# A hybrid attention and pooling step: h by column chunks, four resident weight blocks, w_out split by chunks

## The reference

```python
mod = silu(c) @ w_ada + b_ada                 # shift, scale, gate: 3 x 1024 for each sequence
h = layer_norm(x) * (1 + scale) + shift
q, k, v, g_attn, u, g_pool = split(h @ w_in)  # w_in: 1024 x 2304
q, k = rope(q), rope(k)
o_attn = windowed attention with sinks        # 8 q heads, 2 kv heads, own chunk of 64 and 2 before it
o_pool = (trailing means of u over 2/4/8/16 rows - u) @ w_pool * pool_scale
mixed = concat([o_attn * silu(g_attn), o_pool * silu(g_pool)])
y = mixed @ w_out                             # w_out: 1024 x 1024
out = layer_norm(alpha * x + gate * y) * ln_g + ln_b
```

## Time and profile before

| | |
|---|---|
| Median of 3 runs | 482.06 us (481.42 to 482.42) |
| Span of the profiled execution | 479.1 us (its own time is given by this span alone) |
| PE | busy 447.9 us (93%), 2598 matmuls |
| PE weight loads | 376.8 us (79%) |
| VectorE | 279.3 us (58%) |
| ScalarE | 129.8 us (27%) |
| GpSimd | 118.4 us (25%) |
| Chain that ended last | PE 83%, DVE 9%, ACT 2%, issue 2%, DMA 2% |
| DMA | 46.30 MB, 97 GB/s over the span, 418 GB/s at most |

### The profile page before, as it was taken

One profiled execution on the slowest core, in us unless ns is written; L12 is line 12 of the kernel. 1 busy time (PEld: TensorE's weight loads), 2 busy tenths in 40 slices (PEclk: granted clock), 3 DMA queues, 4 the chain that ended last, 5 costly groups with the idle time before them and its releaser, 6 DMA issues.

```text
span 479.1 us, 6605 instructions
## 1 busy us (share of the span) xinstructions
PE 447.9 (93%) x2598; PEld 376.8 (79%) x2598; DVE 279.3 (58%) x524; ACT 129.8 (27%) x307; POOL 118.4 (25%) x83
## 2 busy tenths in 40 slices
...
GB/s 308 415 418 274 219 0 1 219 2 275 44 46 131 45 44 7 49 46 1 50 8 46 5 45 10 41 51 0 183 16 73 88 89 88 89 88 90 88 98 79
DMA packets 22545, 46.30 MB, mean 97 GB/s; under 512 B 11089, under 2 KB 13649, under 8 KB 21202
## 3 DMA queue, kind: packets, MB, share of 16 engines
...
...
## 4 chain that ended last, share of the span: by engine, by line
PE 83%; DVE 9%; ACT 2%; issue 2%; DMA 2%; POOL 0%; SPq 0%; DVEq 0%; POOLq 0%
PE proj_ps L579 15%; PE proj_ps L581 14%; PE proj_ps L580 14%; PE proj_ps L706 6%; PE proj_ps L707 6%; PE proj_ps L708 6%; PE s_ps L612 3%; PE t_ps L640 2%; PE o_ps L662 2%; PE o_ps L663 2%; PE s_ps L515 2%; DMA xs<-x_all 2%; DVE wo_lo L1126 2%; PE t_ps L535 2%; DVE xnT L989 2%
## 5 line engine op out<-in xcount | busy, mean ns | idle before, releaser
L579 PE MATMUL proj_ps<-h_hi,w_hi 128*128 128x384 f32 x400 | 139.2, 348 | 0.3 <-DVE rt L1024 0.3
L581 PE MATMUL proj_ps<-h_hi,w_lo 128*128 128x384 f32 x400 | 135.0, 338 | 0.0
L580 PE MATMUL proj_ps<-h_lo,w_hi 128*128 128x384 f32 x400 | 135.0, 338 | 0.0
L1250 POOL TENSOR_TENSOR w_lo<-w_raw,w_hi 128x1024 fp32r<-128x1024 f32 x16 | 41.3, 2584 | 160.2 <-ACT w_hi L802 160.2
L579 PEld LDWEIGHTS proj_ps<-h_hi,w_hi 128*128 128x128 f32 x400 | 75.7, 189 | 4.9 <-issue 2.2
L580 PEld LDWEIGHTS proj_ps<-h_lo,w_hi 128*128 128x128 f32 x400 | 75.8, 189 | 0.9
L581 PEld LDWEIGHTS proj_ps<-h_hi,w_lo 128*128 128x128 f32 x400 | 75.6, 189 | 0.0
L706 PE MATMUL proj_ps<-wo_hi,m_hi 128*128 128x512 f32 (+1 forms) x152 | 58.9, 388 | 3.0 <-DVE wo_lo L1126 3.0
L708 PE MATMUL proj_ps<-wo_hi,m_lo 128*128 128x512 f32 (+1 forms) x152 | 58.4, 384 | 0.0
L707 PE MATMUL proj_ps<-wo_lo,m_hi 128*128 128x512 f32 (+1 forms) x152 | 58.4, 384 | 0.0
L1046 DVE SCALAR_TENSOR_TENSOR mixed<-th,proj_ps 128x384 f32<-128x384 f32 x24 | 13.3, 554 | 57.0 <-ACT th L816 57.0
...
## 6 DMA issues: line engine op xcount, KB each, us to landing
w_raw<-w_in SPq DMA_DIRECT2D x18, 512.0 KB, 4.8
...
xs<-x_all SPq DMA_DIRECT2D x9, 512.0 KB, 9.1
xf<-x_all SPq DMA_DIRECT2D x9, 512.0 KB, 4.1
...
y_out<-yr SPq DMA_DIRECT2D x8, 512.0 KB, 2.9
wo_raw<-w_out SPq DMA_DIRECT2D x4, 512.0 KB, 3.3
wo_rest<-w_out SPq DMA_DIRECT2D x4, 512.0 KB, 8.9
```

Of the source, the lines that this page charges most:

```text
L579: pe.matmul(bank[:, 0:CW], w_hi[:, w, k, :], hi, start=(k == 0), stop=False)
L580: pe.matmul(bank[:, 0:CW], w_hi[:, w, k, :], lo, start=False, stop=False)
L581: mm = pe.matmul(bank[:, 0:CW], w_lo[:, w, k, :], hi, start=False, stop=(k == KT - 1))
L1250: pool.tensor_tensor(w_lo[:, b % 2], w_raw[:, b % RAW], w_hi[:, b % 2].bitcast(F32), ALU.subtract).then_inc(wlo_done, 1)
```

## The change

Five things:

1. The two parts of h lie in one tensor `hl`, chunk after chunk (in a chunk: half, part, slice), where they lay in two tensors over all columns. The early modulation slabs are placed to fit.
2. w_in blocks: four high parts are resident, and the low part is written over the raw block. A buffer is refilled when the last unit of block b-4 is done; `W_SPLIT` says after which unit ScalarE splits a block.
3. Loads: slabs 2 and 3 and blocks 2 and 3 come ahead of x tiles 6 to 8.
4. The order: units 4 to 7 are gates of chunks 0 and 1, and chunk 2 of k and v comes as units 8 and 9. Tiles 6 to 8 are transposed after units 4 and 5. The lists of the engines are written to suit; GpSimd makes 2 low parts of h where it made 5.
5. w_out is loaded into the memory of h, slices 0 to 2 when chunk 0 of h has had its last use, 3 to 5 with chunk 1, 6 and 7 with chunk 2; the low part is written over the raw one. Slices 0 to 4 are split before and between the last units. The first two tiles for the residual (`xf`) are loaded before.

The diff, cut to its core:

```diff
-    for c in range(NCH):
+    for c in range(2):
         units += [("k", 0, c), ("v", 0, c)]
-    units += [("ga", j, c) for j in range(4) for c in range(NCH)]
+    units += [("ga", j, c) for j in range(2) for c in range(2)]
+    units += [("k", 0, 2), ("v", 0, 2), ("ga", 0, 2), ("ga", 1, 2)]
+    units += [("ga", j, c) for j in range(2, 4) for c in range(NCH)]
...
+W_SPLIT = {LAST_UNIT[b - RAW] + 1: b for b in range(RAW, NBLK)}
...
-POOL_LOW = [(0, 0), (0, 2), (1, 2), (2, 0), (2, 2)]
+POOL_LOW = [(2, 1), (2, 3)]
...
-POOL_WO = (3, 4)
+POOL_WO = (2, 5)
+WO_CHUNK = [0, 0, 0, 1, 1, 1, 2, 2]
...
-    h_hi = place("h_hi", [P, KT, TOK], F32R, at=r_h)
-    h_lo = place("h_lo", [P, KT, TOK], F32R, at=r_h + KT * TOK * 4)
-    wo_hi = place("wo_hi", [P, KT, D], F32R, at=r_h)
-    wo_lo = place("wo_lo", [P, KT, D], F32R, at=r_h + KT * TOK * 4)
+    hl = place("hl", [P, NCH, 2, 2, KT // 2, CW], F32R, at=r_h)
+    wo = place("wo", [P, KT, 2, D], F32R, at=r_h)
+    wo_raw = place("wo_raw", [P, KT, 2, D], at=r_h)
...
+    wada = [place(f"wada{i}", [P, KT, 512], at=r_h + o * CW * 4) for i, o in enumerate((0, 11, 24, 35))]
...
+    w_lo = place("w_lo", [P, RAW, KT, P], F32R, at=r_raw)
...
+    w_hi = place("w_hi", [P, RAW, KT, P], F32R, at=r_hl)
...
-                    sp.wait_ge(whi_done, b - RAW + 1)
-                    sp.wait_ge(wlo_done, b - RAW + 1)
+                    sp.wait_ge(unit_done, LAST_UNIT[b - RAW] + 1)
                 sp.dma_start(w_raw[:, b % RAW], w_in[b]).then_inc(ld_w[b % RAW], 16)
             def load_w_out(k):
-                if k < RAW:
-                    sp.wait_ge(whi_done, NBLK + k - RAW + 1)
-                    sp.wait_ge(wlo_done, NBLK + k - RAW + 1)
-                elif k == RAW:
-                    sp.wait_ge(s_done, NQ)
-                sp.dma_start(w_out_raw(k), w_out[k]).then_inc(ld_wo[k], 16)
+                sp.wait_ge(unit_done, LAST_USE[WO_CHUNK[k]] + 1)
+                sp.dma_start(wo_raw[:, k, 1, :], w_out[k]).then_inc(ld_wo[k], 16)
+            def load_xf(t):
+                if t >= 2:
+                    sp.wait_ge(r_done, 2 * (t - 1))
+                sp.dma_start(xf[:, t % 2, :], x_all[t]).then_inc(ld_xf[t % 2], 16)
...
+            load_x(3)
             load_w(0)
+            load_x(4)
             load_w(1)
-            load_x(3)
-            load_x(4)
             load_x(5)
+            load_ada(2)
+            load_ada(3)
+            load_w(2)
+            load_w(3)
+            sp.dma_start(cosT[:], cos_d).then_inc(ld_cs, 16)
+            sp.dma_start(sinT[:], sin_d).then_inc(ld_cs, 16)
             load_x(6)
             load_x(7)
             load_x(8)
...
-            for k in range(RAW, KT):
+            for k in range(KT):
                 load_w_out(k)
-            sp.wait_ge(unit_done, LAST_PROJ + 1)
...
-            ada(1, low)
             x_transpose(2)
-            ada(1, high)
             select(0)
+            ada(1)
             select(1)
             unit(0, low)
+            unit(1, low)
             x_transpose(3)
-            unit(1, low)
             x_transpose(4)
             x_transpose(5)
             ada(2)
-            x_transpose(6)
             select(2)
-            ada(3, low)
             unit(2, low)
-            ada(3, high)
-            x_transpose(7)
+            ada(3)
+            unit(3, range(0, 2))
             select(3)
-            x_transpose(8)
-            unit(3, low)
+            unit(3, range(2, 4))
             for n in range(4):
                 unit(n, high)
-            after = {6: [(v_transposes, 0), (v_transposes, 1)], 7: [(ada, 4), (v_transposes, 2), (v_transposes, 3)],
-                     8: [(v_transposes, 4), (v_transposes, 5)], 11: [(ada, 5)]}
+            after = {4: [(x_transpose, 6)], 5: [(x_transpose, 7), (x_transpose, 8)],
+                     10: [(v_transposes, 0), (v_transposes, 1)], 11: [(ada, 4), (v_transposes, 2), (v_transposes, 3)],
+                     12: [(v_transposes, 4), (v_transposes, 5)], 15: [(ada, 5)]}
...
-                if b >= 2:
-                    act.wait_ge(unit_done, LAST_UNIT[b - 2] + 1)
-                act.activation(w_hi[:, b % 2], w_raw[:, b % RAW], ACT.Copy).then_inc(whi_done, 1)
+                if b >= RAW:
+                    act.wait_ge(unit_done, LAST_UNIT[b - RAW] + 1)
+                act.activation(w_hi[:, b % RAW], w_raw[:, b % RAW], ACT.Copy).then_inc(whi_done, 1)
...
             evac_ada(2)
+            h_high(1, (0, 1))
+            evac_ada(3)
+            h_high(0, (2, 3))
+            h_high(1, (2, 3))
+            w_high(2)
+            evac_unit(1)
+            w_high(3)
+            evac_unit(3)
+            normalise(6)
             normalise(7)
-            h_high(1, (0, 1))
+            evac_unit(4)
+            normalise(8)
             evac_xt(6)
-            normalise(8)
-            evac_ada(3)
+            evac_unit(5)
             evac_xt(7)
             evac_xt(8)
-            h_high(0, (2, 3))
-            h_high(1, (2, 3))
-            evac_unit(1)
-            h_high(2)
-            evac_unit(3)
-            w_high(2)
-            evac_unit(5)
-            w_high(3)
-            after = {7: 4, 11: 5}
-            for n in range(6, NU):
+            h_high(2, (0, 1))
+            evac_unit(6)
+            h_high(2, (2, 3))
+            evac_unit(7)
+            after = {11: 4, 15: 5}
+            for n in range(8, NU):
                 b = block_of(n)
                 evac_unit(n)
                 if n in after:
                     evac_ada(after[n])
                 if n == NU - 1:
-                    for k in range(1, 6):
+                    wo_high(5)
+                if UNITS[n] == ("z", GROUPS[3], 0):
+                    mixed_high(0)
+                    for k in range(3):
                         wo_high(k)
+                if n == LAST_PROJ:
+                    wo_high(3)
+                    wo_high(4)
                 for i in SLOTS.get(n, []):
                     slot(i)
-                if b is not None and LAST_UNIT[b] == n and b + 2 < NBLK:
-                    w_high(b + 2)
-                if UNITS[n] == ("z", GROUPS[3], 0):
-                    mixed_high(0)
-                if n == LAST_PROJ:
-                    wo_high(0)
+                if n in W_SPLIT:
+                    w_high(W_SPLIT[n])
...
-            w_low(0)
             modulation(0)
-            w_low(1)
+            x_stats(3)
             modulation(1)
             h_ops(0, (0, 1))
-            x_stats(3)
-            h_low(0, (1,))
+            w_low(0)
+            h_low(0, (0, 1))
             x_stats(4)
+            w_low(1)
             x_stats(5)
+            modulation(2)
+            h_ops(1, (0, 1))
+            h_low(1, (0, 1))
+            modulation(3)
+            h_ops(0, (2, 3))
+            h_low(0, (2, 3))
+            h_ops(1, (2, 3))
+            h_low(1, (2, 3))
+            w_low(2)
+            evac_unit(0)
+            evac_unit(2)
             x_stats(6)
             x_stats(7)
+            evac_unit(4)
             x_stats(8)
-            h_ops(1, (0, 1))
-            modulation(2)
-            h_low(1, (0, 1))
-            evac_xt(6)
-            evac_xt(7)
-            modulation(3)
-            h_ops(0, (2, 3))
-            evac_xt(8)
-            h_ops(1, (2, 3))
-            h_low(0, (3,))
+            evac_unit(5)
             h_ops(2, (0, 1))
-            h_low(1, (3,))
             h_samples(0)
+            h_low(2, (0,))
             h_ops(2, (2, 3))
             h_samples(1)
-            evac_unit(0)
-            h_low(2, (1, 3))
-            evac_unit(2)
-            evac_unit(4)
-            after = {6: [0, 1], 7: [2, 3], 8: [4, 5]}
-            for n in range(6, NU):
+            h_low(2, (2,))
+            evac_unit(6)
+            evac_unit(7)
+            after = {10: [0, 1], 11: [2, 3], 12: [4, 5]}
...
+                if UNITS[n] == ("z", GROUPS[3], 0):
+                    wo_low(0)
+                    wo_low(1)
+                if n == NU - 1:
+                    wo_low(3)
+                    wo_low(4)
                 for i in SLOTS.get(n, []):
                     slot(i)
-            for k in range(5, KT):
-                wo_low(k)
+            wo_low(6)
+            wo_low(7)
...
-            inv_std(0)
-            inv_std(1)
-            inv_std(2)
-            h_low(0, (0,))
-            inv_std(3)
-            inv_std(4)
-            inv_std(5)
-            inv_std(6)
-            inv_std(7)
-            inv_std(8)
-            h_low(0, (2,))
-            h_low(1, (2,))
-            h_low(2, (0, 2))
-            for b in range(2, NBLK):
-                s = (b - 12) // 2 if b < NBLK - 1 else 3
-                if b >= 12 and (b % 2 == 0):
-                    window_sums(s, 0)
+            for t in range(6):
+                inv_std(t)
+            w_low(3)
+            for t in range(6, TILES):
+                inv_std(t)
+            h_low(2, (1, 3))
+            for b in range(4, 14):
```

(55 more changed lines are left out.)

101 lines of the change are left out of this document (39 added, 62 removed).

## The result

| | median of 10 runs, us | lowest to highest |
|---|---|---|
| before | 481.36 | 480.94 to 482.46 |
| after | 484.55 | 483.01 to 485.88 |

The ratio is 1.0061 (95% interval 1.0044 to 1.0077): 2.9 us slower. The forecast was 482.6, its range 479.3 to 485.9. The profiled execution of after is one of its faster ones (483.32, span 481.5 against 479.1), so the traces differ by 2.4. They split it at the start of output tile 0: the front lost 6.2, the tail won 3.7.

What follows compares the result with a forecast made beforehand. PE's work plus its holes was taken to bound the kernel. Span 479.1 + 3.7 (front) - 3.2 (tail) = 479.6, plus 2.96 from span to median, gave 482.6 us; range 479.3 to 485.9, the forecast's own 481.0 to 484.2.

Steps and rivals of the forecast that it cites:

- rival 2: Front, slower: PE's clock falls twice, on units 6 and 7 or unit 1's low half, each 1.5 us; 485.6, chance 0.18.
- Those named as wrong: Signs against the forecast: x6's transposes without a wait, front under +1, or waits for wo over 1.5 us.
- those named as right: Signs: x waits near 64 (over 3 us) and 73, k unit 26.9, high half near 51, chunk 2 under 1.5, tile 0 in 12.
- Front, to the first k unit: First k unit starts at 26.85 against 26.27, +0.6, with VectorE's w_low(0) after the four h operations.
- To the end of unit 3: Unit 2 at 43.35 after 1.95 idle, high half at 51.3, ending at 59.85 with x6 to x8 still to come.
- Units 4 to 6: x6 waits 3.65 behind VectorE's list (GpSimd's lock 1.67 of it), x7 waits 2.0; unit 6 ends at 81.6, +2.7.
- Unit 8: k of chunk 2 waits for the last low part of h and ends at 90.9 instead of 89.9, +1.0.
- Middle: After the front: waits for the four resident blocks and late modulation slabs stay hidden; without that cover 1 to 3 us.
- Tail: Output tile 0: earlier w_out parts remove PE's waits, only part 6 late by 0.6; -3.2, or -1.2 if engines collide.
- Rival 3: Tail, slower: VectorE and GpSimd lock each other over w_out's low parts, -1.0 instead of -3.2; 484.8, chance 0.13.
- Rival 1: Front, faster: no lock on the first k evacuation, x5's evacuations close up; front +0.7 to +1.2, 479.9, chance 0.27.
- Rival 4: Whole kernel: the change meets no wait of PE, front and tail cancel exactly; 482.1, inside the forecast's joint chance of 0.42.

Runs made afterwards that it cites:

- e7: After with statistics of x6 to x8 ahead of modulation(3) and low parts of blocks 0 and 1 earlier on VectorE; 477.56 us, ratio 0.9936 to before.
- e3: After with filler transposes that nobody reads where PE was idle, ahead of unit 0, unit 2 and x6; 482.83 us, ratio 1.0030 to before.
- e10: After with x6 evacuated ahead of the normalisation of x8 on ScalarE; 484.32 us, ratio 1.0048 to before.
- e11: After with x6 to x8 loaded ahead of weight blocks 2 and 3, statistics early, x6 and x7 transposed in PE's gaps; 477.39 us, ratio 0.9906 to before.
- e5: After with the front order of before, ScalarE's high part of block 2 waiting for the second k evacuation; 478.29 us, ratio 0.9939 to before.
- e9: After with GpSimd's low part of block 3 behind the powers of x6 to x8; 482.85 us, ratio 1.0023 to before.

## Why the prediction was right, and by how much its terms were off

The shape held: the front loses, the tail wins less than that. The size of the change did not: +3.7 - 3.2 = +0.5 was forecast, +6.2 - 3.7 = +2.5 is in the traces, and the ratio says 2.9. 484.55 lies above the forecast's own 481.0 to 484.2; it is inside the range only because this was stretched to rival 2. There is some luck as well: the forecast started from 482.06, the median of three runs, and ten runs of before gave 481.36, so 0.7 of the miss doesn't show in the time. The signs were mixed. Those named as wrong did not come; of those named as right the first k unit, unit 8 and tile 0 came, PE's waits for normalised x tiles lead its list, but x6's wait stands at 67 to 70 and not near 64, there is no second listed wait (x7 starts at 78.07 with none), and the high half of unit 0 was 2.8 late. Step by step:

- *Front, to the first k unit*: +0.6 forecast, +0.96 measured (27.23 for 26.27). The cause named, w_low(0) behind the h operations, is the releaser in the row. That undoing it gains nothing in the end (e7) the forecast did not see.
- *To the end of unit 3*: the high half of unit 0 at 51.3 forecast, 54.10 measured. 0.8 was there at unit 2 (44.13 for 43.35), and 1.54 is the clock (e3). This is the term that failed most: I had the idle of 1.95 in front of unit 2 in my own walk and let no clock fall follow it.
- *Units 4 to 6*: x6's wait 3.65 forecast, 3.17 measured; its start is 2.5 late, all inherited from above. The lock was put at 1.67 and is 1.40. The clock fell behind the wait, as forecast; "hidden by x7's wait" was nearly so: 0.8 of it showed, because the two end together (e10, e3). At the mark +2.7 forecast, +5.8 measured.
- *Unit 8*: +1.0 forecast. The unit starts at 88.67 with no wait listed. From the mark to tile 0 the trace has +0.4 with the same 1770 matmuls in both kernels: 0.27 of it is in the distances between the products with h, 0.14 in those of one attention product, and after has no wait of over 0.3 us there. Since unit 6 ended 3.1 later than forecast, chunk 2's h was in time; in e11, where it was not later, the wait is there (1.38).
- *Middle*: 0 forecast, and no wait in the list, 269.63 busy of 270 (the +0.4 above is spread over it). e5 puts the new storage, ring and loads at about 0.8, where I counted nothing.
- *Tail*: -3.2 forecast, -3.74 measured, all there was. Part 6, which I had late by 0.6, was in time: VectorE began it at 374.77 and takes 1.2, PE came to it at 376.4 (367.98 + 6 x 1.41). Rival 3 fell: the engines did lock each other (5.22 for two), off the path.

Rival 2 had the mechanism of the miss, the clock falling twice, and its sign came (a granted clock under 1 at 45 to 49 and up to 76); the places it named, unit 1 and units 6 and 7, were others. Its 485.6 is nearer to 484.55 than the forecast is. Rival 1's first condition, that the lock doesn't bite, would have been worth 1.8 (e9). Rival 4 fell, since front and tail both move a lot and don't cancel (+6.2 and -3.7).
